# Differential attention with all scores of a step on four row groups, inverse sums folded into the turns, and the first turn ahead of the values

## The reference, cut to what matters

```
def attend(q, k, v):                         # differential attention, "A"
    s = einsum('bqhcd,bkhcd->bhcqk', q, k) * (A_QK ** -0.5)      # c = 0, 1; A_QK = 32
    p = softmax(s, axis=-1)
    a = p[:, :, 0] - lam * p[:, :, 1]
    return einsum('bhqk,bkhd->bqhd', a, v)

# neighbourhood attention, "B": one product over 64 numbers a head, a bias on 512 of the keys
s_win = einsum('brqhd,brikhd->brhqik', qg, k_rows) * scale + bias
s_ctx = einsum('brqhd,bkhd->brhqk', qg, kc) * scale
p = softmax(concatenate([s_win, s_ctx], axis=-1), axis=-1)
ol = einsum(p_win, v_rows) + einsum(p_ctx, vc)
```

## Time and profile before

| | us |
|---|---|
| three runs | 2427.86, 2428.32, 2429.92 |
| median | 2428.32 |
| the profiled execution, its own time | 2428.85 |
| its span | 2427.0 |
| PE busy in it | 2283.8 (94%) |
| DVE busy | 978.6 (40%) |
| ACT busy | 540.9 (22%) |
| POOL busy | 188.1 (8%) |
| attention: first maximum to the end of the last values | 258.94 to 421.24 |

### The profile page before, as it was taken

The page is one execution under the profiler, slowest core; times in us unless marked ns, Lnnn a source line. Parts: engine busy times, 40 slices in busy tenths (PEclk is TensorE's granted clock), DMA queues, the critical chain, the costliest instruction groups (busy, mean ns, idle before and its releaser), DMA issues.

```text
span 2427.0 us, 28782 instructions
## 1 busy us (share of the span) xinstructions
PE 2283.8 (94%) x10062; PEld 1606.8 (66%) x10063; DVE 978.6 (40%) x1800; ACT 540.9 (22%) x1133; POOL 188.1 (8%) x181
## 2 busy tenths in 40 slices
PE   8999899867798998999999999999999999999999
PEld 2554455422333477778888888566676788888888
DVE  5532688530000135725335432444244534335421
ACT  3201466411111144522111100131231212111100
POOL 0000436011111000000000002202010000000000
PEclk9999999878899999989999999999999999999999
DMA  9220153559787921012222221312112122222230
GB/s 350 84 97 30 43 189 136 231 192 381 270 334 261 353 107 52 27 53 78 87 86 82 75 104 54 129 44 86 61 60 78 35 105 79 88 87 89 75 120 19
DMA packets 81023, 298.02 MB, mean 123 GB/s; under 512 B 8989, under 2 KB 8989, under 8 KB 80430
## 3 DMA queue, kind: packets, MB, share of 16 engines
q1 hardware_dynamic: 75102, 271.26, 31.7%
q0 software_dynamic: 5840, 25.67, 2.9%
HBM read 282.73 MB, written 14.16 MB: 122 GB/s over the span
## 4 chain that ended last, share of the span: by engine, by line
PE 84%; DVE 7%; issue 3%; ACT 3%; SPq 2%; DMA 2%; DVEq 0%; POOL 0%; ACTq 0%; POOLq 0%
PE products L1589 41%; PE products L988 8%; PE products L1419 6%; PE products L1212 6%; PE products L1494 3%; PE products L1437 3%; PE products L1753 2%; PE products L1671 2%; PE products L1328 1%; PE products L1544 1%; DVE tiny L2531 1%; PE products L1227 1%; SPq L828 1%; DMA weights_and_work<-in_experts 1%; ACT weights_and_work L1960 1%
## 5 line engine op out<-in xcount | busy, mean ns | idle before, releaser
L1589 PE MATMUL products<-normed,weights_and_work 128*128 128x264 f32 (+1 forms) x1520 | 348.7, 384 | 0.0
L1589 PEld LDWEIGHTS products<-normed,weights_and_work 128*128 128x128 f32 x1520 | 288.1, 190 | 50.7 <-issue 5.3
L1419 PE MATMUL products<-weights_and_work 128*64 128x512 f32 x768 | 181.1, 632 | 47.3 <-DMA weights_and_work<-in_experts 46.6
L1589 PE MATMUL products<-weights_and_work,mixed 128*128 128x256 f32 (+1 forms) x800 | 182.3, 382 | 0.8 <-ACT weights_and_work L1844 0.8
L1844 ACT ACTIVATE weights_and_work<-products 128x256 f32<-128x256 f32 (+4 forms) x225 | 99.4, 456 | 371.5 <-PE products L1589 156.4
L1419 PEld LDWEIGHTS products<-weights_and_work 128*64 128x64 f32 x768 | 65.6, 146 | 161.1 <-issue 160.0
L1589 PEld LDWEIGHTS products<-weights_and_work,mixed 128*128 128x128 f32 x800 | 151.8, 190 | 24.4 <-ACT weights_and_work L1844 1.6
L1589 PE MATMUL products<-weights_and_work 128*128 128x256 f32 (+1 forms) x672 | 151.0, 386 | 7.2 <-DVE residual L3248 5.2
L1589 PE MATMUL products<-weights_and_work,normed 128*128 128x264 f32 (+1 forms) x704 | 155.6, 382 | 0.0
L1589 PE MATMUL products<-normed,mixed 128*128 128x264 f32 (+1 forms) x672 | 154.1, 382 | 0.0
L1589 PEld LDWEIGHTS products<-weights_and_work 128*128 128x128 f32 x672 | 128.9, 192 | 28.0 <-issue 7.3
(11 more groups left out here) (565 smaller groups left out, 2974.0 us busy)
## 6 DMA issues: line engine op xcount, KB each, us to landing
weights_and_work<-in_weights SPq DMA_DIRECT2D x301, 512.0 KB, 4.3
weights_and_work<-in_experts SPq DMA_DIRECT2D x192, 512.0 KB, 5.3
results<-normed SPq DMA_DIRECT2D x8, 512.0 KB, 7.1
residual<-in_x POOLq DMA_DIRECT2D x1, 2048.0 KB, 15.7
weights_and_work<-in_dft_half POOLq DMA_DIRECT2D x1, 2048.0 KB, 13.3
token_rows<-mixed SPq DMA_DIRECT2D x4, 512.0 KB, 3.1
normed<-results SPq DMA_DIRECT2D x4, 512.0 KB, 7.1
mixed<-results SPq DMA_DIRECT2D x4, 512.0 KB, 8.6
```

The source lines that it names most:

```text
L1419: m = pe.matmul(ps[UNIT * b:UNIT * (b + 1), side, :], job_t[:, k, UNIT * b:UNIT * (b + 1)], expert_w[b][:, s, at:at + 512], start=(k == 0) ...
L1589: m = pe.matmul(bank(p, n), left(k), right(k), start=(fresh and k == 0), stop=(k == kt - 1), skip_group_check=True)
```

## The change

- `scores`: the copies `alone` and their buffers are gone. A's two products use 32 rows of the array each, and B's product of 64 rows is made as two products of 32 rows that are added in PSUM; on the four row groups of the array, nine products in all, with two waits of PE for its own products (`scores_halfway`, `scores_ending`) where two groups would write the same bank. A and B are announced together, by the last one.
- DVE no longer scales 768 columns by an inverse sum: it scales the identity, 128 columns (`inverse_a`, `inverse_b`). `joined` keeps one instruction, p0 minus lambda * sum0/sum1 * p1.
- `turn` is a product with that diagonal instead of a transpose.
- PE turns A of step s and makes the first `out_1` ahead of the values of s - 1. `o_sum` comes a step later, ahead of the turn.
- ACT copies A's turn ahead of `exps(s + 1, "A")`. B's probabilities and A's turned ones get two buffers.

```
@@ plan
+        if s - 1 in SUMMED_AT:
+            r["o_sum", SUMMED_AT[s - 1]] = b.take(5)
+        turned(s, "A")
         if s > 0:
             r["PV", s - 1] = b.take(6)
-        for kind in "AB":
-            r["T", s, kind] = [b.take(5), b.take(6)]
+        turned(s, "B")
@@ PE scores
                     fill(a)
-                    pe.wait_ge(q_alone, s + 1)
-                    for c in range(2):
-                        for at, width in ((0, 512), (512, 256)) if c == 0 else ((0, 256), (256, 512)):
-                            m = pe.matmul(wide(a, 2 * NKEY)[:, NKEY * c + at:NKEY * c + at + width], aq_alone[:, h % 2, c],
-                                          ak[:, h // 2, at:at + width], start=True, stop=True)
-                    finish(a, m)
                     fill(b_)
-                    for at, width in ((0, 512), (512, 256)):
-                        m = pe.matmul(wide(b_, NKEY)[:, at:at + width], bq_alone[:, 1 - h % 2], bk[:, h // 2, at:at + width],
-                                      start=True, stop=True)
-                    finish(b_, m)
+                    first(1, 0, 256).then_inc(halfway, 1)
+                    m = first(0, 0, 512)
+                    second(0, 0, 512, True, False).then_inc(halfway, 1)
+                    second(1, 512, 256, True, False).then_inc(halfway, 1)
+                    first(1, 256, 512).then_inc(ending, 1)
+                    pe.wait_ge(halfway, 3 * s + 3)
+                    first(0, 512, 256).then_inc(ending, 1)
+                    second(1, 0, 256, False, False)
+                    second(0, 512, 256, False, True).then_inc(ending, 1)
+                    pe.wait_ge(ending, 3 * s + 3)
+                    finish(a, second(1, 256, 256, False, True), 2)
@@ PE turn
-                            m = pe.transpose(ps[:, p.bank, (kt % 4) * P:(kt % 4 + 1) * P], of[:, kt * P:(kt + 1) * P], ident)
+                            m = pe.matmul(ps[:, p.bank, (kt % 4) * P:(kt % 4 + 1) * P], of[:, kt * P:(kt + 1) * P], inverse,
+                                          start=True, stop=True)
@@ PE loop
                     scores(s + 1)
+                    if s - 1 in SUMMED_AT:
+                        summed(SUMMED_AT[s - 1])
+                    turn(s, "A")
+                    out_1(s, 0)
                     if s > 0:
                         weigh(s - 1)
-                    turn(s, "A")
-                    out_1(s, 0)
                     turn(s, "B")
                     out_1(s, 1)
-                    if s in SUMMED_AT:
-                        summed(SUMMED_AT[s])
@@ ACT loop
-                    if s + 2 < len(STEPS):
-                        read(act, r["scores", s, "B"])
-                        alone(s + 2)
+                    turned(s, "A")
                     exps(s + 1, "A")
                     if s > 0:
                         weighed(s - 1)
-                    turned(s, "A")
+                    exps(s + 1, "B")
+                    turned(s, "B")
                     if s in SUMMED_AT:
                         squares_a(SUMMED_AT[s])
-                    exps(s + 1, "B")
-                    turned(s, "B")
@@ DVE
-                    link(ts(inv[:, 1:2], inv[:, 1:2], neg_lam, None, ALU.mult))
+                    link(ts(inv[:, 1:2], inv[:, 1:2], neg_lam, sums[:, 0:1], ALU.mult, ALU.mult))
-                    ts(joined_a, prob_a[:, 0], inv[:, 0:1], None, ALU.mult).then_inc(prob_scaled, 1)
-                    dve.wait_ge(prob_scaled, s + 1)
-                    stt(joined_a, prob_a[:, 1], inv[:, 1:2], joined_a, ALU.mult, ALU.add).then_inc(prob_ready, 1)
+                    ts(inverse_a, ident, inv[:, 0:1], None, ALU.mult)
+                    stt(joined_a, prob_a[:, 1], inv[:, 1:2], prob_a[:, 0], ALU.mult, ALU.add).then_inc(prob_ready, 1)
-                    ts(scaled_b, prob_b, row_inv[:, s % 2, 2:3], None, ALU.mult).then_inc(b_ready, 1)
+                    ts(inverse_b, ident, row_inv[:, s % 2, 2:3], None, ALU.mult).then_inc(b_ready, 1)
```

More of the change, by code:

```diff
@@ L223, in scores, with turned @@
             r["scores", s, "B"] = b.take(3, 4)
+    def turned(s, kind):
+        r["T", s, kind] = [b.take(5), b.take(6)]
     scores(0)
@@ L1222, in scores @@
                     a, b_ = r["scores", s, "A"], r["scores", s, "B"]
+                    o = DH * (h % 2)
                     fill(a)
[L1224 to L1230 removed]
@@ new lines, in first, with second @@
+                    def first(c, key, width):
+                        return product(wide(a, 2 * NKEY), NKEY * c + key, aq, ak, o + 32 * c, key, width)
+                    def second(half, key, width, start, stop):
+                        return product(wide(b_, NKEY), key, bq, bk, DH - o + 32 * half, key, width, start, stop)
+                    first(1, 0, 256).then_inc(halfway, 1)
+                    m = first(0, 0, 512)
+                    if s == 0:
+                        begin(m)
+                    second(0, 0, 512, True, False).then_inc(halfway, 1)
@@ L1929, in projections @@
                 for t in range(NKT):
[L1930 to L1933, removed]
-                        for s in range(2):
-                            alone(s)
-                    copy(r["v"][t], vals[:, t], bank(r["v"][t]).rearrange("p (a c) -> p a c", a=2))
-            def alone(s):
-                t, h = STEPS[s]
-                at, o = slice(t * P, (t + 1) * P), DH * (h % 2)
-                for c in range(2):
-                    rows_ = slice(o + 32 * c, o + 32 * c + 32)
-                    act.activation(aq_alone[rows_, h % 2, c], aq[rows_, h // 2, at], ACT.Copy)
-                rows_ = slice(DH - o, 2 * DH - o)
-                act.activation(bq_alone[rows_, 1 - h % 2], bq[rows_, h // 2, at], ACT.Copy).then_inc(q_alone, 1)
+                    copy(r["v"][t], vals[:, t], bank(r["v"][t]).rearrange("p (a c) -> p a c", a=2))
             def attentions():
@@ L1965, in turned @@
                         n = 4 if j == 0 else 2
-                        copy(p, prob_t[:, "AB".index(kind), 4 * j:4 * j + n], bank(p, n * P).rearrange("p (k q) -> p k q", k=n))
+                        copy(p, prob_t[:, s % 2 if kind == "A" else 2, 4 * j:4 * j + n], bank(p, n * P).rearrange("p (k q) -> p k q", k=n))
                 def weighed(s):
```

36 lines of the change are left out of this document (17 added, 19 removed).

## The result

| | runs, us | median |
|---|---|---|
| before, on the same chip | 2427.86 to 2429.92, 4 runs | 2428.91 |
| changed | 2447.98, 2449.99, 2453.24, 2456.58 | 2451.61 |

The ratio is 1.0097, interval 1.0082 to 1.0111: slower, by 22.7 us. The forecast was slower by 5.2, with a range that ended at 2449. The side was right, the size was not.

The account below looks back on a forecast made before the run. Attention bound by PE's own work in odd steps (8.7 us) and the bank 7 wait in even ones (11.35); -4.3 + 5.6 + 3.4 = +4.7, taken as +5.2 on 2428.85, so 2434.0 us, range 2425 to 2449.

Parts of the forecast that it names:

- The wait for bank 7: Attention's even steps: PE waits some 2.6 us before the first out_1 for DVE's copy behind both maxima, seven times.
- The clock: Rival, chance 0.07: PE runs slow after each of seven bank 7 waits, 1.7 us each, +12, giving 2446.
- The sum: Attention's total: -4.3 to the third maximum, +5.6 to the sixteenth, +3.4 after; +4.7, taken as +5.2 us.
- the new wait of 2.6 is near the second: Clock rival's argument: after 2.66 us idle the old scores took 2.82 against 2.74; after 3.81, rows were slow.
- The prices: Unit costs on PE: 0.43 us per 512-column pass, A's or B's turn 1.40, out_1 0.86, values 1.56, scores 2.4.
- The odd step: Attention steps without the bank 7 wait: PE's own work sets them, 8.7 us.
- The even step: Attention steps 2, 4, ..., 14: with the wait for bank 7, 11.35 us, seven times.
- The head-sum step: Three odd steps where a head sum ahead of A's turn adds 1.7 us: 10.4 us.
- Row groups that slow each other: Rival, chance 0.19: four row groups don't overlap fully, scores 2.9 to 3.4 us, +8 to +16, 2442 to 2450.
- Scores at 2.1: Rival, chance 0.2: weights and waits hidden, scores 0.3 us less in 15 or 16 steps, 2429.4, no change.
- Bank 7 not waited for: Rival, chance 0.09: even steps take 8.7 us, 2.65 less seven times; 2417 after POOL's costs.
- the ring: Attention's old chain of waits per step: A's scores, maximum, exponentials, copy, turns, both out_1; 9.32 us.

Follow-up runs that it names:

- copy_first: The changed kernel with DVE's copy out of bank 7 moved ahead of both maxima: 2424.3 us, ratio 0.9988 to the kernel before.
- order_alone: The kernel before with only the change's new order on PE and ACT, old scores and transposes kept: 2436.0 us, ratio 1.0037.
- filled_both: The changed kernel with products of zeros on PE in the bank 7 waits and twelve more between the first and second scores: 2444.1 us, ratio 1.0067.
- diagonals_alone: The kernel before with only the turns changed, to products with diagonals: 2435.4 us, ratio 1.0034.
- order_copy: The kernel before with the new order and DVE's bank 7 copy ahead of both maxima, old scores and transposes: 2421.1 us, ratio 0.9972.
- scores_order_copy: The kernel before with row-group scores, the new order and the bank 7 copy ahead of both maxima, turns still transposes: 2420.1 us, ratio 0.9969.
- scores_alone: The kernel before with only the changed scores, nine products on four row groups: 2438.1 us, ratio 1.0036.
- diagonal_b: Row-group scores, new order and early bank 7 copy, with a diagonal product for the second component only, against the kernel before: 2421.1 us, ratio 0.9973.
- diagonal_a: Row-group scores, new order and early bank 7 copy, with a diagonal product for the first component only, against the kernel before: 2420.7 us, ratio 0.9971.
- filled_even: The changed kernel with five products of zeros on PE in each even step's wait for bank 7: 2447.0 us, ratio 1.0079.

## Why the prediction was wrong in size

**The wait for bank 7: right.** Idle 2.60 us before `out_1`, forecast some 2.6; seven times; DVE's copy behind both maxima releases it; copy_first shows its worth, and the other way round order_alone shows that it hits the old scores and transposes as well.

**The clock: the step that failed.** The sum had nothing for falls of the granted clock. They stood beside it as a rival with a chance of 0.07, at 1.7 us for each wait for bank 7. The runs show 9.3 us in the profile (of 13.9 missed there) and about 10 in the median (of 17.5). They come in three places:

- 3.1 us at the start. The sum made this wait itself: it let the scores of step 1 wait for B's exponential, 2 us longer, and did not ask what 5.98 us of idling do to the rows behind. filled_both puts 3.1 of the 3.5 us by which m2 came late (279.15 for 275.6) on that.
- 3.0 us (1.6 and 1.4) directly behind the new waits of 2.60, two of the seven.
- 3.2 us in two head-sum steps, beginning in A's turn behind a wait of 0.77. That these come from the wait for bank 7 is not shown. For it: they are gone when that wait is filled. Against it: copy_first and three other kernels without that wait have them too.

The reasoning was "the new wait of 2.6 is near the second" (of two old waits, the one of 2.66 us after which the scores were not slow). One case without a fall was taken for a rule. In diagonals_alone the same wait of 2.66 has a fall behind it, 4.09 for 2.82. At 1.9 to 2.6 us of idling both happen, fall and no fall, in one execution. The rival would also have been wrong in its mechanism, which was one fall a wait for bank 7. This should have stood in the sum as a term with a range.

**The prices, 5.8 us.** The odd step is 8.99 for 8.7: scores 2.75 on PE (352.68 to 355.43 in the chain) for 2.49 with the change of form, each turn 1.53 for 1.40, the first of them with the other 0.09 in it, values 1.46 for 1.56. The even step is 11.83 for 11.35: 4.10 from the maximum to `out_1` for 3.98, 1.09 from there to the values for 0.86, values 1.47 for 1.56, B's turn 1.53 for 1.40, and 2.78 to the next maximum for 2.69. The head-sum step is 10.81 for 10.4. Over the steps that is 0.9 + 2.9 + 1.2 (four, six, three), and 0.4 at each end, the first with the 0.3 by which m0 came later. With the clock's 9.3 it makes 15.1, less the 0.5 that had been put in for POOL and the 0.8 by which the stretch behind attention was shorter: 13.8, where the spans want 19.1 - 5.2 = 13.9. The forecast of 2434.0 also took as the median what had been added to a profiled execution 0.5 above it, too little to matter.

**The other rivals.** Row groups that slow each other: not seen; eighteen passes, 5.2 us one after another at 0.43 for 512 columns and 0.215 for 256, went through in 2.75 with two waits inside, for 2.9 to 3.4 in the rival. The first passes of the four groups start within 0.02 us of one another, and a pass of 512 columns follows another of its group after 0.43 (353.14 and 353.57). What was too cheap are the two waits: from the last column to the next product's start 0.27 and 0.35, for 0.16 + 0.05. The Trainium skill (TensorE: Matmul & The Clock Gate, Part 3, Measured speedup) would have given 3.07 times; its 2442 came nearer to the result than the forecast, but by luck, since the time was lost elsewhere. Scores at 2.1: false. Bank 7 not waited for: false. Its price was nearly right, 2.83 a time for 2.65, but the 2417 without the wait was not: copy_first gives 2424.3, with two dearer turns, the start and one fall of the clock that it had not counted.

**Where each part's gain went.** Row-group scores: off the ring before, then idle time. The order: 7.2 us of gain together with the copy ahead of the maxima (order_copy), turned into a loss by where that one copy stood. The copy moved alone, in the kernel before, was not run; there PE lost nothing to it in the step of the earlier trace rows. Diagonals: 0.88 us of PE a turn for 0.45 of DVE, in a kernel whose quiet steps PE sets: scores_order_copy is 4.2 us faster than copy_first in the median, their intervals just touching, and differs by the diagonals and by where some buffers lie.

## What to carry to other kernels

When work is moved ahead on one engine, follow each bank that it passes to the instruction that releases it, on the other engine's queue, and move that too: the same order was worth -7.2 us with the copy first and +8.0 without. Price a new idle stretch of PE not by its length alone but also by what may come at a lower clock behind it, and list every one that the change makes, at the start too; filling it with products of zeros is a quick way to find out how much. Shorter work on an engine pays only where that engine sets the step.

## What the hardware showed that was not expected

- The granted clock fell after idle stretches of 1.87 us (scores_alone), 2.19 us (order_alone) and 2.66 us (diagonals_alone), and did not after others of 1.87, 2.19, 2.60 and 2.66. A fall cost 1.5 to 1.6 us in a step, and 3.1 us after 5.98 us of idling. What decides it between the two is open; no run changed the length of the wait alone.
- In head-sum steps of the new order PE waits 0.77 us, and its idle time is under 1 us in sum. With row-group scores the clock fell in seven of 21 such steps: two of the changed kernel, one of copy_first (PE busy 11.5 of 12.5 us, 1.6 us more), one of scores_order_copy, two of diagonal_b, one of diagonal_a, none of the six in filled_even and filled_both. With the old scores (order_alone, order_copy) it fell in none of six behind the same wait. Whether the row groups have a part in it was not tested, and one profile each can't tell it. One such turn of order_copy, at its usual pace:

```profile
315.29 0.85 PE L1248 MATMUL products<-const_sb,weights_and_work 128*128 128x128 f32 x6 [0.77 <-ACT weights_and_work L1848]
```

- After a wait of 2.6 us at a clock of 1.00 the next two products take 1.10 for 1.02 and the next stage starts 0.23 later than behind products that follow on. After 0.88 us of waiting (filled_even, 359.29) they take 1.10 too.
- A product with a diagonal takes 2.3 times as long as a transpose of the same block (1.53 in the chain of the changed kernel, 0.66 before, six blocks), 2 x 0.128 a block for 0.11.
